# Stick-breaking attention: the causal mask of 28 steps set by GpSimd instead of by TensorE

## The reference

```
for i in range(T // Q_BLOCK):                       # 8 blocks of 128 queries
    z = einsum('bqhd,bshd->bhqs', qb, kb) * scale
    strict = s_idx < t_idx                          # keys before the query only
    log_beta = log_sigmoid(z)
    log_1mb = where(strict, log_sigmoid(-z), 0.0)
    tail = cumsum(log_1mb, axis=3, reverse=True) - log_1mb
    a = where(strict, exp(log_beta + tail), 0.0)
    out = einsum('bhqs,bshd->bqhd', a, vb)
```

## Time and profile before

| | |
|---|---|
| time, 3 runs | 1177.46, 1179.66, 1179.71 us; median 1179.66 |
| the profiled execution | 1177.58 us, of which the span from first to last instruction is 1175.8 us |
| granted TensorE clock | 0.995 of full speed over the span |
| PE busy | 1148.6 us |
| DVE, ACT, POOL busy | 841.1, 741.7, 288.5 us |

### The profile page before, as it was taken

The page is one execution under the profiler, slowest core; times in us unless marked ns, Lnnn a source line. Parts: engine busy times, 40 slices in busy tenths (PEclk is TensorE's granted clock), DMA queues, the critical chain, the costliest instruction groups (busy, mean ns, idle before and its releaser), DMA issues.

```text
span 1175.8 us, 17197 instructions
## 1 busy us (share of the span) xinstructions
PE 1148.6 (98%) x6160; PEld 918.5 (78%) x6160; DVE 841.1 (72%) x967; ACT 741.7 (63%) x907; POOL 288.5 (25%) x252
## 2 busy tenths in 40 slices
PE   8999999999999989999989999999999999999997
PEld 6898787866766657777878788888888888888886
DVE  5521212257777796777787999889888898898893
ACT  6633222366655793334557787887877877877873
POOL 2400000010100011333242244334433432332322
PEclk9999999999999999999989999999999999999999
DMA  8155433010100241665788999999999999999992
GB/s 277 46 209 203 162 151 117 1 54 19 37 19 18 100 137 52 251 228 220 283 304 327 367 401 398 382 397 371 390 385 388 382 389 370 401 370 377 399 373 47
DMA packets 71029, 288.18 MB, mean 245 GB/s; under 512 B 16224, under 2 KB 23409, under 8 KB 46402
## 3 DMA queue, kind: packets, MB, share of 16 engines
q1 hardware_dynamic: 51538, 238.30, 52.6%
q0 software_dynamic: 14064, 30.31, 9.0%
q10 hardware_dynamic: 5376, 18.88, 4.1%
HBM read 248.82 MB, written 54.80 MB: 258 GB/s over the span
## 4 chain that ended last, share of the span: by engine, by line
PE 57%; DMA 1%; DVE 1%; issue 1%; POOL 0%; ACT 0%; POOLq 0%; DVEq 0%; ACTq 0%
PE banks L781 17%; PE banks L783 17%; PE banks L782 17%; PE banks L1159 2%; PE banks L1192 1%; PE banks L1063 1%; DMA rows_dram<-v_row,dest 1%; PE banks L993 1%; PE banks L1006 1%; DMA xb<-rows_dram 0%; PE banks L1054 0%; PE banks L973 0%; DMA out_dram<-y_row,scatter_row 0%; PE banks L1043 0%; DVE ew_l L1694 0%
## 5 line engine op out<-in xcount | busy, mean ns | idle before, releaser
L1694 DVE TENSOR_TENSOR ew_l<-raw,ew_h 128x2048 fp32r<-128x2048 f32 x192 | 430.7, 2284 | 0.0
L1518 ACT ACTIVATE ew_h<-raw 128x2048 fp32r<-128x2048 f32 x192 | 365.2, 1920 | 55.3 <-PE banks L783 48.2
L781 PE MATMUL banks<-ew_h,xb_h 128*128 128x512 f32 x520 | 206.3, 397 | 1.9 <-issue 1.6
L783 PE MATMUL banks<-ew_h,xb_l 128*128 128x512 f32 x520 | 203.1, 391 | 0.0
L782 PE MATMUL banks<-ew_l,xb_h 128*128 128x512 f32 x520 | 202.7, 390 | 0.0
L1843 DVE TENSOR_TENSOR_SCAN tails<-tails 128x512 f32<-128x512 f32 (+3 forms) x96 | 94.9, 1030 | 42.9 <-ACT tails L1479 42.9
L781 PE MATMUL banks<-win_h,u_h 128*128 128x512 f32 (+1 forms) x312 | 119.3, 382 | 1.4 <-DVE u_l L1694 1.4
L783 PE MATMUL banks<-win_h,u_l 128*128 128x512 f32 (+1 forms) x312 | 115.5, 370 | 0.0
L782 PE MATMUL banks<-win_l,u_h 128*128 128x512 f32 (+1 forms) x312 | 115.3, 370 | 0.0
L781 PEld LDWEIGHTS banks<-ew_h,xb_h 128*128 128x128 f32 x520 | 98.2, 189 | 21.8 <-issue 1.7
L783 PEld LDWEIGHTS banks<-ew_h,xb_l 128*128 128x128 f32 x520 | 97.8, 188 | 20.9
(11 more groups left out here) (267 smaller groups left out, 1961.4 us busy)
## 6 DMA issues: line engine op xcount, KB each, us to landing
raw<-in_expert_w_gate SPq DMA_DIRECT2D x64, 1024.0 KB, 7.8
raw<-in_expert_w_down SPq DMA_DIRECT2D x64, 1024.0 KB, 7.2
raw<-in_expert_w_up SPq DMA_DIRECT2D x64, 1024.0 KB, 10.9
rows_dram<-zero_rows ACTq DMA_DIRECT2D x8, 2048.0 KB, 7.3
win_raw<-in_w_in SPq DMA_DIRECT2D x16, 512.0 KB, 5.3
x_in<-in_x SPq DMA_DIRECT2D x8, 512.0 KB, 10.7
raw<-in_w_out SPq DMA_DIRECT2D x4, 1024.0 KB, 5.0
h_row<-in_x SPq DMA_DIRECT2D x8, 512.0 KB, 6.8
```

What stands on the lines that cost most here:

```text
L781: mm(ps, lh, rh, start=start, stop=False)
L783: return mm(ps, ll, rh, start=False, stop=stop)
L1518: A(ew_h[slot % SPLIT][:, :], raw[raw_slot][:, :], ACT.Copy).then_inc(ew_h_ready, 1)
L1694: return V.tensor_tensor(dst, src, high.bitcast(fp32), SUB)
```

## The change

The top steps from 0 to 39 (28 of them: 0 to 15, and 16, 18, ... 38) leave out the two masking products. GpSimd sets the diagonal 128 columns instead, for both heads in one instruction, once in `tails` to 1 (behind ACT's `tails`) and once in `beta` to 0 (behind ACT's `beta`): 56 new instructions on 128 partitions by 256 columns. DVE's first scan of such a step waits for the first of them, its product for the second. The top steps 40, 42, 44 and 46 stay as they were. GpSimd's program now has the masks in the order of the steps, and `z_l` number b (1 to 5) stands behind the masks of step `Z_SPLIT[b]`.

```
+        for n, u in enumerate(steps_z):
+            u["set"] = u["top"] and n <= FILL_LAST
+        SETS = [sum(u["set"] for u in steps_z[:n + 1]) for n in range(NZ)]
...
-            for b in range(FILL_UNITS // 2):
+            def low_z(b):
                 pool.wait_ge(z_h_ready, b + 1)
                 nc.gpsimd.tensor_tensor(z_l[b % 2][:, :, :], z_raw[b % 2][:, :, :], z_h[b % 2][:, :, :].bitcast(fp32),
                                         SUB).then_inc(z_l_ready, 1)
+
+            def mask(n):
+                u = steps_z[n]
+                if not u["set"]:
+                    return
+                for ready, block, fill in ((c_done, tails[u["row"] % 2][:, :, T - P:T], 1.0),
+                                           (beta_done, beta[n % 3][:, :, u["w"] - P:u["w"]], 0.0)):
+                    pool.wait_ge(ready, n + 1)
+                    nc.gpsimd.affine_select(out=block, in_=block, compare_op=ALU.is_gt, fill=fill, base=0,
+                                            pattern=[[0, 2], [-1, P]], channel_multiplier=1).then_inc(masked_z, 1)
+
+            low_z(0)
+            for n in range(FILL_LAST + 1):
+                mask(n)
+                for b in range(1, FILL_UNITS // 2):
+                    if Z_SPLIT[b] == n:
+                        low_z(b)
...
-                if u["top"]:
+                if u["top"] and not u["set"]:
                     for h in range(2):
                         last = mm(z[h][:, u["w"] - P:u["w"]], ident_b[:, :], causal_neg[:, :], start=False, stop=True,
                                   skip_group_check=True)
...
-                    dve.wait_ge(c_done, n + 1)
+                    if u["set"]:
+                        dve.wait_ge(masked_z, 2 * SETS[n] - 1)
+                    else:
+                        dve.wait_ge(c_done, n + 1)
                     for h in range(2):
                         part = row[:, h, c0:c1][:, ::-1]
                         last = V.tensor_tensor_scan(out=part, data0=part, data1=part,
                                                     initial=1.0 if u["top"] else row[:, h, c1:c1 + 1], op0=MUL, op1=ALU.min)
-                    last.then_inc(scanned, 1)
                     gates_of(n, 0)
-                    dve.wait_ge(scanned, n + 1)
-                    dve.wait_ge(beta_done, n + 1)
+                    link(last)
+                    if u["set"]:
+                        dve.wait_ge(masked_z, 2 * SETS[n])
+                    else:
+                        dve.wait_ge(beta_done, n + 1)
```

More of the change, by code:

```diff
@@ L274, in hybrid_block_kernel @@
                                                               sem("g_decay"), sem("g_exp"), sem("g_kdec"))
-        qk_done, c_done, beta_done, scanned, a_done = sem("qk_done"), sem("c_done"), sem("beta_done"), sem("scanned"), sem("a_done")
+        qk_done, c_done, beta_done, masked_z, a_done = sem("qk_done"), sem("c_done"), sem("beta_done"), sem("masked_z"), sem("a_done")
         a_turned_sb, prob_ready, pv_done = sem("a_turned_sb"), sem("prob_ready"), sem("pv_done")
```

## The result

| | before | after |
|---|---|---|
| median (lowest to highest), 11 runs each, same chip | 1177.58 us (1176.88 to 1180.44) | 1180.92 us (1179.60 to 1182.01) |
| profiled execution | 1177.58 us | 1180.92 us |
| span | 1175.8 us | 1179.2 us |
| granted clock over the span | 0.995 | 0.992 |

The ratio is 1.0023, with a 95% interval of 1.0015 to 1.0031. A later comparison of the same two kernels gave 1.0015 (1.0006 to 1.0025). So the change makes the kernel slower by 2 to 3 us, about two tenths of a per cent. The forecast was 1181.1 us, but the two profiles show that its mechanism accounts for little of this.

A forecast was written before the change was run, and what follows sets the result against it. The prediction took PE to set the pace in steps 4 to 39 and DVE in 40 to 47. Start +2.3, step 24 +0.8 and other pairs -1.7 gave +1.4 on 1179.66: 1181.1 us, range 1177.4 to 1183.4.

The forecast's parts named there:

- What a pair costs PE: Steps 0 to 39: removing a step's two masking products saves PE 0.075 us, 2.1 us for 28 pairs.
- What a mask costs the chain: Masked steps: select 0.45 us plus hand-overs 0.08 and 0.14; first scan 0.67 us behind ACT instead of 0.03.
- The turn of the second mask: Every masked step: the second mask comes during DVE's scans and adds a turn of about 0.35 us between them.
- The start: Steps 0 to 2: `z_l` and masks delay step 1's product to 250.0; PE wanted it at 247.70, +2.3 us.
- neither side runs two in a row while the other waits: DVE and GpSimd on SBUF: they take turns at instruction boundaries; the second mask adds about 0.35 us a step.
- The other pairs: Steps 4 to 39 without step 24: 23 removed pairs at 0.075 us give -1.7 us.
- the cover of 2.5 us: Steps 4 to 39: PE reaches the transposes at least 2.5 us after DVE's product, hiding the 0.8 us delay.
- the rival in which gain and loss cancel: Start +1.0, step 24 +0.5, pairs -1.7: -0.2 in sum, 1179.5 us; chance 0.30.
- The failed step: Steps 0 to 39: PE's gain or loss there moves everything behind by the same amount; total +1.4 us.
- the removal shows in full: Rival: no pile-up at the start, masks slip into DVE's idle time; -2.1 to -1.5, 1177.8 us; chance 0.09.
- the unit ends at steps 20 and 30: Slower rival: PE also waits for gate products there, +0.4 each; total +3.2, 1182.9 us; chance 0.16.

The follow-up runs named there:

- e1_no_mask: Kernel before without the 28 masking pairs and nothing in their place, the mask left out there; 1178.19 us, ratio 0.9989 to the kernel before.
- e7_fewer: Kernel after with GpSimd masks in 23 steps only (0 to 3 and 24 keep products), `z_l` number 1 behind step 5; 1177.62 us, 0.9989 of before.
- e2_both: Kernel after with the masking products still there, so masks are set twice; 1180.96 us, ratio 1.0022 to the kernel before.
- e3_zl_late: Kernel after with `z_l` number 1 behind the masks of step 5 instead of step 1; 1179.87 us, ratio 1.0007 to the kernel before.
- e6_warm_after: Kernel after with 25 identity transposes filling three of PE's waits in the hand-over to the experts; 1179.19 us, ratio 0.9998 to the kernel before.
- e11_load_late: Kernel after with one 1 MB expert weight load (piece 7) issued about 10 us later; 1177.46 us, ratio 0.9990 to the kernel before.
- e4_double: Kernel before with the masking pair issued twice in the 16 top steps 12 to 38; 1182.83 us, ratio 1.0035 to the kernel before.
- e5_warm_before: Kernel before with 25 identity transposes filling three of PE's waits in the hand-over to the experts; 1178.15 us, ratio 0.9990 to the kernel before.
- e8_fewer_warm: Kernel after with 23 GpSimd-masked steps, `z_l` number 1 behind step 5, and 25 transposes in the hand-over's waits; 1176.87 us, 0.9978 of before.
- e9_double3: Kernel before with the masking pair issued twice in steps 34, 36 and 38 only; 1179.34 us, ratio 1.0002 to the kernel before.
- e10: Kernel after, unchanged, measured again beside more runs of the kernel before; 1181.72 us, ratio 1.0015 to the kernel before.
- e12_all: e8_fewer_warm with the 1 MB weight load (piece 7) issued about 10 us later; 1176.66 us, ratio 0.9982 to the kernel before.

## Why the prediction was right, and where it wasn't

The number was right by luck. 1181.1 stood on 1179.66, the median of three runs; the kernel before then measured 1177.58, 2.1 us less. The forecast step was +1.4 us and the measured one is +3.3 by the medians, or 1.8 to 2.7 by the two ratios. A base too high and a step too small nearly cancel in 1180.92. Inside the step, the attention's losses came out smaller than forecast, and a loss came in that the prediction had excluded.

- *What a pair costs PE* was right: 0.077 us by e1_no_mask, 0.073 by e7_fewer, 0.065 between the kernel after and e2_both, against 0.075.
- *What a mask costs the chain* was right for the select and the hand-overs. The groups of the kernel after give the means:

```profile
L631 POOL TENSOR_SCALAR_AFFINE_SELECT beta<-beta 128x256 f32<-128x256 f32 x28 | 22.5, 804 | 5.8 <-ACT beta L1502 5.7
...
L631 POOL TENSOR_SCALAR_AFFINE_SELECT tails<-tails 128x256 f32<-128x256 f32 x28 | 13.2, 472 | 100.8 <-ACT tails L1499 100.8
```

  These means mix selects that ran alone with others. A select with no DVE instruction beside it took 0.41 us (forecast 0.45), and of the 28 of `beta` eight took that too, while most that fell beside a scan took 1.03 (forecast 0.8). At step 24 the first scan starts 0.58 us behind ACT (0.67).
- *The turn of the second mask* was too large. At step 24, from ACT's end to DVE's product's end it is 4.34 us after and 3.63 before: +0.71, of which about 0.15 is the second mask's turn, not 0.35. With the scores released 0.2 earlier, DVE is 0.5 us later relative to PE, not 0.8. That gave +0.5 at step 24 in place of +0.8. The Trainium skill ("SBUF — State Buffer", section "Who interferes with whom") has the two block each other, and they do: the select of `beta` takes twice as long beside scans. It says that the one that issues first holds the other for its whole instruction; it doesn't say who goes next when both have more to do.
- *The start* cost 1.35 us, not 2.3. `z_l` did hold step 1's scans. But one of the two scans was over before it (0.28 us), `z_l` ended 0.17 us earlier, and the two masks of step 2 didn't come between the scans (0.72): scan and product followed `z_l` directly. The product took 0.44 us instead of 0.3. 250.0 less 1.03 is 248.97, and it ended at 248.99. The reading "neither side runs two in a row while the other waits" was the mis-sized step; the earlier trace rows showed a case of it and no rule. e3_zl_late shows the place.
- *The other pairs.* Starts of step 40: 1.35 + 0.5 - 0.27 = 1.6 us gained on 23 pairs, 0.070 each (forecast 1.7). No other wait for DVE appeared in steps 0 to 39, so the cover of 2.5 us was enough. Together the attention gives +0.27: the rival in which gain and loss cancel (-0.2) was nearer than the forecast.
- *The failed step* is the sentence "What PE gains or loses in them moves everything behind by the same amount". It holds to 578 us. In the hand-over PE waits for rows that come by DMA, and the clock falls behind such waits. This added 2.45 us in the profile, 0.9 by the trip and the rest, by what e6_warm_after takes away, by the half clock; e11_load_late takes away the trip's part and most of the low-clock runs. In the same way e4_double turned 1.8 us into 4.1 (0.35%). The sentence failed in a second place too, the 0.8 us that e1_no_mask lost between 434 and 442.
- *The rivals.* That the removal shows in full fell, and so did the unit ends at steps 20 and 30.

The loss lies in the hand-over: both profiles of the kernel after show it, and filling PE's waits or moving one load there takes most of it away. That GpSimd's selects are what makes the trip long is excluded: e4_double has none and a long trip (e1_no_mask too, with the reservation above), e2_both and e7_fewer have them and a short one. Scatter is excluded by 22 of 22. Still open is why a program has a trip of 13.2 to 13.4 us (before, e2, e5, e7, e8, e9) or of 14.0 to 14.6 (after, e1, e3, e4, e6, e10). It isn't the delay alone, since e9_double3 and the kernel after start step 40 within 0.05 us of each other; how the rows' packets fall among those of the weight loads would fit, but no run separates it from the rest. Open as well is what sets the length of the half clock. A long trip came with 13.7 us in every profile without filling, but the kernel before, e2_both, e7_fewer and e9_double3, with the same three waits of PE within 0.1 us, have 6.8, 13.7, 6.8 and 3.4 us.

## What to carry to other kernels

Work that is taken from a full engine must be followed to the next place where that engine waits for a DMA: a change of 0.3 us before it can come out as 3, so compare the two traces by the start of the same instruction in each stage, down to the end. Work that is moved to a side engine cost nothing here where 2.5 us of cover existed, and showed at the start and at step 24, where there was none; leave those few steps as they were (e7_fewer), and keep long instructions of the side engine from standing just before a short chain. Where a stage's hand-over leaves the product engine waiting, filling the wait was worth as much here (e5_warm_before, 0.9990) as the masks at their best (e7_fewer, 0.9989).

## What the runs showed of the hardware

- The granted clock's fall at one hand-over lasted 6.8 us in one program and 13.7 in another that differed by 0.27 us up to there; a run with the long stretch takes 1.6 to 2.2 us more. Over the profiles the stretch is 0, 3.4, 6.8, 10.2 or 13.7 us, and not the same for the same waits. It came with waits of PE of at most 1.66 us in the kernel before and 1.0 in e11_load_late. With 25 small transposes in the waits none of 41 runs in four kernels is at 0.994 or less; two of their four profiles have no half clock until the last few us, and two (e8_fewer_warm, e12_all) have 3.4 us. What the transposes cost is not shown: e5_warm_before takes 0.8 us more than the kernel before in its runs above 0.994 (1177.38), but those are picked runs, and at 602 us its profile is 0.5 us ahead.
- A product pair that is doubled costs 0.09 to 0.11 us (e9_double3, e4_double), a pair that is removed gives 0.065 to 0.08.
- One 1 MB load issued 10 us later shortened the rows' way through DRAM by 2.4 us, all of it on the way back.
- Two scans of 128 columns that take 0.73 us alone took 2.92 with a 2.38 us GpSimd subtraction beside them.
